# A decoder layer in float32r halves: the up projection's 512-column matmuls cut into two of 256 with the same weights

## What is computed

```
h = rms_norm(x, attn_norm_g);  proj = h @ w_in                  # 2048 x 11344
o_sb, o_ds = stick-breaking attention, indexed sparse attention  # 8 heads each
merged = sigmoid(g_sb) * (o_sb @ w_branch[:1024]) + sigmoid(g_ds) * (o_ds @ w_branch[1024:])
x = x + merged @ w_out
h = rms_norm(x, ffn_norm_g)
u = causal_depthwise_conv(h @ w_up, conv_w, conv_b)              # w_up: 2048 x 11264
gate, val = split(u, 2)                                          # 5632 columns each
return x + (silu(gate) * val) @ w_down                           # w_down: 5632 x 2048
```

## Time and profile before

| | us |
|---|---|
| median of 3 runs (lowest to highest) | 1439.2 (1438.27 to 1439.45) |
| the profiled execution, its own time | 1438.79 |
| span of its trace, first to last instruction | 1436.8 |
| TensorE (PE) busy | 1429.7 |
| weight loads (PEld) busy | 1224.2 |
| VectorE busy | 1141.6 |
| ScalarE busy | 842.1 |
| GpSimd busy | 448.5 |
| up stage, first to last matmul | 712.2 to 1203.9 |

### The profile page before, as it was taken

One profiled execution on the slowest core, in us unless ns is written; L12 is line 12 of the kernel. 1 busy time (PEld: TensorE's weight loads), 2 busy tenths in 40 slices (PEclk: granted clock), 3 DMA queues, 4 the chain that ended last, 5 costly groups with the idle time before them and its releaser, 6 DMA issues.

```text
span 1436.8 us, 23628 instructions
## 1 busy us (share of the span) xinstructions
PE 1429.7 (100%) x7570; PEld 1224.2 (85%) x7570; DVE 1141.6 (79%) x1532; ACT 842.1 (59%) x1181; POOL 448.5 (31%) x495
## 2 busy tenths in 40 slices
PE   9999999999999999999999999999999999999999
PEld 7888888888888888888888888888888888888887
DVE  6778998986656556889967777778778778999998
ACT  6645667566767766666665455454554545465553
POOL 2310000423232213650015455655556555200000
PEclk9999999999999999999999999999999999999999
DMA  8665665665554555567666666666666665576664
GB/s 261 179 190 173 204 198 186 192 182 173 157 174 146 175 163 184 183 215 238 191 184 182 190 192 188 178 192 191 198 187 182 187 192 189 188 236 206 199 210 147
DMA packets 120919, 272.24 MB, mean 189 GB/s; under 512 B 10672, under 2 KB 10704, under 8 KB 120864
## 3 DMA queue, kind: packets, MB, share of 16 engines
q1 hardware_dynamic: 119936, 269.12, 61.4%
q0 software_dynamic: 896, 2.42, 0.6%
q10 hardware_dynamic: 32, 0.01, 0.0%
HBM read 269.42 MB, written 2.10 MB: 189 GB/s over the span
## 4 chain that ended last, share of the span: by engine, by line
PE 94%; DVE 3%; POOL 1%; issue 1%; ACT 1%; DMA 1%; SPq 0%; DVEq 0%; ACTq 0%; POOLq 0%
PE bank L2071 93%; DVE lo L1658 1%; DVE lo L1203 0%; DMA raw<-in_w_in 0%; POOL u L2035 0%; PE bank L2120 0%; PE bank L2332 0%; ACT hi L633 0%; PE bank L2373 0%; DVE conv L1610 0%; POOL conv L2038 0%; ACT hT L650 0%; DVE y L1748 0%; DVE whole L1700 0%; DMA raw<-in_w_down 0%
## 5 line engine op out<-in xcount | busy, mean ns | idle before, releaser
L1094 DVE TENSOR_TENSOR lo<-raw,hi 128x1024 fp32r<-128x1024 f32 (+1 forms) x343 | 446.5, 1307 | 167.2 <-ACT hi L633 166.4
L633 ACT ACTIVATE hi<-raw 128x1024 fp32r<-128x1024 f32 (+1 forms) x343 | 360.3, 1053 | 272.9 <-PE bank L2071 268.4
L2071 PE MATMUL bank<-h2T,hi 128*128 128x512 f32 x1408 | 483.3, 394 | 0.0
L2071 PE MATMUL bank<-h2T,lo 128*128 128x256 f32 x1408 | 376.9, 278 | 0.0
L2071 PEld LDWEIGHTS bank<-h2T,hi 128*128 128x128 f32 x1408 | 257.9, 188 | 53.5
L2071 PE MATMUL bank<-hT,hi 128*128 128x512 f32 (+1 forms) x784 | 272.8, 395 | 0.5 <-DVE lo L1094 0.5
L2071 PEld LDWEIGHTS bank<-h2T,lo 128*128 128x128 f32 x1408 | 264.5, 188 | 7.8
L2071 PE MATMUL bank<-hT,lo 128*128 128x256 f32 (+1 forms) x784 | 212.6, 281 | 0.0
L2035 POOL TENSOR_TENSOR u<-u,rms_row 128x256 f32<-128x256 f32 x88 | 120.8, 1373 | 184.9 <-DVE u L1600 165.9
L2071 PE MATMUL bank<-hi,ffT 128*128 128x512 f32 x576 | 177.4, 389 | 0.0
L2071 PEld LDWEIGHTS bank<-hT,hi 128*128 128x128 f32 (+1 forms) x784 | 143.9, 187 | 30.1 <-DVE lo L1094 0.8
(11 more groups left out here) (298 smaller groups left out, 2022.6 us busy)
## 6 DMA issues: line engine op xcount, KB each, us to landing
raw<-in_w_up SPq DMA_DIRECT2D x176, 512.0 KB, 3.7
raw<-in_w_in SPq DMA_DIRECT2D x160, 512.0 KB, 3.6
raw<-in_w_down SPq DMA_DIRECT2D x88, 512.0 KB, 4.5
raw<-in_w_branch SPq DMA_DIRECT2D x32, 512.0 KB, 3.7
raw<-in_w_out SPq DMA_DIRECT2D x24, 512.0 KB, 5.1
raw4h<-in_w_in SPq DMA_DIRECT2D x8, 512.0 KB, 3.6
raw5h<-in_w_in SPq DMA_DIRECT2D x8, 512.0 KB, 4.1
y<-in_x SPq DMA_DIRECT2D x4, 512.0 KB, 6.4
```

Source lines behind the costliest of these rows:

```text
L633: act.activation(hi[s][:, 0:width], raw[s][:, 0:width], ACT.Copy)\
L1094: dve.tensor_tensor(lo[s][:, 0:width], raw[s][:, 0:width], hi[s][:, 0:width].bitcast(f32), ALU.subtract)\
L2071: return pe.matmul(o, l, r, start=start, stop=stop, skip_group_check=True)
```

## The change

In `cols_chunk` the matmul of `hi` weights is issued in pieces of `width` columns with the same stationary operand: each piece reads its own columns of `src` and adds to the same columns of the bank. Only the up stage passes 256; all other users keep 512, that is one piece. In the up stage each pair becomes three matmuls of 256 columns. Only the very first piece of a bank clears it (`at_ == 0`); the semaphores go up after the last piece.

```
-            def cols_chunk(c, slot, src, kts, bank, first, last, free, full):
+            def cols_chunk(c, slot, src, kts, bank, first, last, free, full, width=2 * S):
...
                         if not (first and j == 0):
                             mm(bank[ct][:, 0:S], wl[:, j, cs], src[:, kt, 0:S], False, False)
-                        i = mm(bank[ct][:, :], wh[:, j, cs], src[:, kt, :], first and j == 0,
-                               last and j == CK - 1)
+                        for at_ in range(0, 2 * S, width):
+                            i = mm(bank[ct][:, at_:at_ + width], wh[:, j, cs],
+                                   src[:, kt, at_:at_ + width], first and j == 0 and at_ == 0,
+                                   last and j == CK - 1)
...
                         cols_chunk(C_UP + b * CPG + 2 * CPG * n + j + 1, j % SLOTS, h2T,
                                    range(CK * j, CK * (j + 1)), (A, B)[b], j == 0,
                                    j == CPG - 1, (free_a, free_b)[b],
-                                   (col_full, bcol_full)[b])
+                                   (col_full, bcol_full)[b], S)
```

## The result

| | before | after |
|---|---|---|
| median of four runs, us (lowest to highest) | 1438.74 (1438.14 to 1439.45) | 1456.45 (1455.95 to 1458.57) |
| span of the profiled execution, us | 1436.8 | 1454.3 |

The ratio is 1.0127, with a 95% interval from 1.0114 to 1.0139: slower by 17.7 us (16.4 to 20.0). The forecast was 1458.0 us, 18.8 us over the median of 1439.2 known then.

What follows compares the result with a forecast made beforehand. The prediction took TensorE's pace as the bound: 1438.8 us for the profiled execution plus 1408 x 13.3 ns = 18.8 us gave 1457.6, forecast as 1458.0 us because the median runs 0.4 higher; range 1445 to 1463 us.

Steps and rivals of the forecast that it cites:

- What bounds the kernel: Whole kernel: TensorE's pace sets the time, busy 1429.7 of 1436.8 us; the up stage pays any pair's change 1408 times.
- step 1: Up stage: 1408 matmuls of 512 columns become 2816 of 256; one more fixed part of 13.3 ns each, +18.8 us.
- step 2: Up stage: the repeat with the same weights brings its own load and pays 13.3 ns; bounds +9.4 to +23.5 us.
- lower end, 6.7 ns: Price of a repeated-weight matmul, read from two suffix-sum starts 60 ns apart: 1408 x 6.7 = +9.4 us.
- step 3: Up stage: a weight load stays covered by a 256-column matmul, 104 ns against 120; costs nothing.
- steps 4 to 6: Later semaphores, the loop's longer body, the first body's transposes and the down stage: no cost taken; possible loop stall 5 us.
- step 4: Up stage: semaphores rise some 13 ns later per pair; waiters already idle 253, 379, 262 us; VectorE next bound, 113 us away.
- The sum: Whole kernel: the profiled execution's 1438.8 us plus 18.8 gives 1457.6; with the median 0.4 higher, 1458.0 us.
- The stream of one width: Up stage: equal widths reach a lower pace, 113.3 ns a matmul, -9.4 us, 1429.8 us; chance 7%.
- The nearly free repeat: Up stage: repeated weights cost 0 to 2 ns (1439 to 1442 us, 4%) or 2 to 6.7 (to 1448.6 us, 9%).
- the 2.5 ns: Up stage: the skill's fixed part per matmul instead of 13.3 ns, +3.5 us, 1442.7 us; counted with the cheap-repeat rival.
- TensorE short of loads or code: Up stage: load, sequencer or loop code sometimes late at 256-column steps; 130 ns for one of three, 1472 us; chance 7%.

Runs made afterwards that it cites:

- run 2: Against the changed kernel, all up-stage matmuls cut to 128 columns, two of low and four of high weights a pair: 1893.08 us (one run).
- 320-column run: Against the kernel before, both matmuls of a pair at 320 columns instead of 256 and 512, first pairs of a bank whole: 1424.44 us (one run).

## Why the prediction was right, point by point

- **What bounds the kernel** was right. TensorE is busy for all of the up stage in both kernels, its waits for low parts did not grow, and the stages around the change kept their length within 0.2 us.
- **The pace taken apart (step 1)**, 0.4167 ns a column and 13.3 ns a matmul, was right and is now shown at four widths with full loads: 120.0 ns at 256, 146.5 at 320, 173.3 at 384, 226.6 at 512. It has a limit that the prediction didn't give: at 128 and 192 columns a matmul takes 111.7 ns, the load's floor. Where the two meet is an estimate from these numbers, (111.7 - 13.3) / 0.4167 = about 236 columns; no width between 192 and 256 was run.
- **The repeat (step 2)** pays the whole fixed part. The forecast took the right value for it, but its lower end, 6.7 ns, came from a misread row: a start that is recorded ahead of the matmul's turn. The next start would have shown it.
- **The load is covered (step 3)**: true, but by 8 ns. I wrote that it costs nothing because a load with its transpose took 104 ns; that row was misread in the same way as the repeat, and the stream's own floor is 111.7. That the forecast needed only "less than 120" was some luck. Cut once more, to 128 columns, the same stage runs at that floor: 1893 us in run 2.
- **Semaphores, the loop, the rest (steps 4 to 6)**: no wait of TensorE appeared in the up stage, and a loop turn is 384 x 120 ns to within the 10 ns of the view, so the longer body costs nothing. But step 4 misread a row: 253, 379 and 262 us are busy times, of ScalarE, VectorE and GpSimd, and not idle times, and none is SyncE's. Its "next bound, 113 us away" was wrong as well. It took VectorE's busy time for the bound, and the 320-column run met one at 43.6 us a turn, 0.8 us below the 44.40 of before, some 8 us in ten turns. The forecast was safe from this only because the change made TensorE slower.
- **The sum** was 18.8 us, measured 17.7 between the medians and 17.5 between the spans. The mis-sized term is the pace of the kernel before. A turn had 44.40 us, not 128 x 346.7 ns = 44.37, and the first body was slower than 346.7 ns a pair. From 740 to 759 us, nearly its whole val half, it ran at another even pace:

```profile
745.06 0.40 PE L2071 MATMUL bank<-h2T,hi 128*128 128x512 f32 x1
...
746.12 0.40 PE L2071 MATMUL bank<-h2T,hi 128*128 128x512 f32 x1
...
747.18 0.40 PE L2071 MATMUL bank<-h2T,hi 128*128 128x512 f32 x1
```

  Three pairs in 1.06 us, 353.3 ns each. In the changed kernel the same stretch runs at 120.0 ns a matmul. These 54 or so pairs at 6.7 ns make up 0.4 us of what is missing in the first body, which lost 1.1 us where 128 x 13.3 ns = 1.7 was counted; the other 0.2 us were not traced; the ten turns lost 16.8 where 17.1 was counted. The rest, some 0.4 us in the spans, lies in the two stretches around.
- **The rivals.** The stream of one width does settle, at 120.0 ns, exactly even, but not at 113.3: the alternation had cost nothing in the loop, as the two 384-column matmuls show, and some 0.4 us in the first body. The nearly free repeat is out. So are the 2.5 ns that the Trainium skill (TensorE: Matmul & The Clock Gate, Back-to-back issue gap) gives an isolated matmul: every float32r stream with 128-column loads here needs 13.3 or more, once it is longer than the load. TensorE short of loads or code: not at 256 columns; at 128 and 192 the floor of 111.7 ns binds.

## What to carry to other kernels

When TensorE is the bound, count its matmuls as well as its columns: here each float32r matmul with its load costs 13.3 ns over its columns, and cutting one in two adds that price, even with the same weights. No cut tried here was free, and each piece of 128 or 192 columns took 111.7 ns. Before you call an engine the next bound by its busy time, remember the run at 320 columns: the chain of transfers and engines bound at 43.6 us a turn, where the busiest of them was busy for 34. Two long counts of starts, at two widths, are enough to get both terms, but a third width should be looked for before a short one is trusted.

## What was not expected of the hardware

- A matmul behind a short one is recorded as starting 60 ns after it, and seems to wait for its weights within its own record: 0.33 instead of 0.28 us shown, the next start 0.17 instead of 0.12 us away. The distance between two starts is a price only if the next distances are taken with it.
- With stationary operands of 64 or 32 columns a 256-column matmul takes 113.4 ns, not 120.0. A 512-column matmul between such ones gains nothing, and a stream of 512 columns alone takes 230.2 ns, not 226.6.
- A stream of one pattern can keep one of two even paces, 346.7 or 353.3 ns a pair in the kernel before, with nothing waiting. The equal widths (three of 256, two of 384) showed only the faster one in the same place. What chooses between them was not tried.
- With TensorE waiting for more, the rest of the up stage settled at 43.6 us a turn, and VectorE, the busiest of the other engines, was busy for only 34 of them.
